# Broadcasting the decay rows of a Mamba-2 mixer: one float32 matmul over a masked product in place of four fp32r matmuls with a selector

## The reference

```python
def ssd_scan(xh, dt, a, bmat, cmat):        # 16 heads, chunks of l = 128 tokens
    ...
    da = (dt * a).reshape(bsz, nc, l, g, hg).transpose(0, 3, 4, 1, 2)
    a_cs = jnp.cumsum(da, axis=-1)
    causal = jnp.tril(jnp.ones((l, l), dtype=bool))
    seg = a_cs[..., :, None] - a_cs[..., None, :]
    decay = jnp.exp(jnp.where(causal, seg, -jnp.inf))
    ...
    y_diag = jnp.einsum('bghcls,bcsghp->bclghp', cb[:, :, None] * decay, x)
    ...
    out_decay = jnp.exp(a_cs).transpose(0, 3, 4, 1, 2)
    y_off = jnp.einsum('bclgn,bcghpn->bclghp', cc, prev) * out_decay[..., None]
```

## Time and profile before

| | |
|---|---|
| median of 3 runs | 3178.87 us (3178.72 to 3179.73) |
| profiled execution | 3178.72 us, span 3177.1 us |
| PE busy | 3030.4 us (95%) |
| DVE busy | 2357.7 us (74%) |
| ACT busy | 1511.5 us (48%) |
| mean granted clock of PE | 0.981 |

### The profile page before, as it was taken

The page is one execution under the profiler, slowest core; times in us unless marked ns, Lnnn a source line. Parts: engine busy times, 40 slices in busy tenths (PEclk is TensorE's granted clock), DMA queues, the critical chain, the costliest instruction groups (busy, mean ns, idle before and its releaser), DMA issues.

```text
span 3177.1 us, 50852 instructions
## 1 busy us (share of the span) xinstructions
PE 3030.4 (95%) x16136; PEld 2531.2 (80%) x16136; DVE 2357.7 (74%) x5175; ACT 1511.5 (48%) x2636; POOL 215.8 (7%) x348
## 2 busy tenths in 40 slices
PE   6999999989998899999999999998999999999998
PEld 4888887769787788877888888877788778888887
DVE  4777787456556766997777777777679977777776
ACT  3222222345753663196555555446532955555544
POOL 0000000000000000092000000000001910000000
PEclk8999999999999999999999999999999999999999
DMA  6333333123222333403555555523343145555553
GB/s 260 108 121 105 114 112 114 68 83 133 79 84 103 107 134 120 157 29 137 191 186 185 186 190 192 196 95 107 133 133 133 41 143 187 185 185 189 191 188 132
DMA packets 73920, 439.61 MB, mean 138 GB/s; under 512 B 7184, under 2 KB 8720, under 8 KB 31824
## 3 DMA queue, kind: packets, MB, share of 16 engines
q1 hardware_dynamic: 71136, 419.15, 38.0%
q0 software_dynamic: 2528, 18.02, 1.6%
q10 hardware_dynamic: 144, 0.98, 0.1%
HBM read 437.08 MB, written 1.05 MB: 138 GB/s over the span
## 4 chain that ended last, share of the span: by engine, by line
PE 77%; DVE 14%; ACT 3%; DVEq 2%; issue 2%; DMA 1%; ACTq 0%; POOL 0%; SPq 0%
PE bank L469 16%; PE bank L471 16%; PE bank L470 16%; PE bank L2323 10%; PE bank L2325 5%; PE bank L1505 2%; DVE arena L2509 2%; PE bank L2286 1%; PE bank L875 1%; DVE arena L2438 1%; DVE arena L2431 1%; DVE arena L2432 1%; PE bank L1225 1%; PE bank L864 1%; PE bank L1243 1%
## 5 line engine op out<-in xcount | busy, mean ns | idle before, releaser
L448 ACT ACTIVATE peer_r<-wring 128x512 fp32r<-128x512 f32 x1280 | 797.6, 631 | 807.1 <-PE bank L471 525.6
L453 DVE TENSOR_TENSOR peer_r<-wring,peer_r 128x512 fp32r<-128x512 f32 x1280 | 869.7, 691 | 413.2 <-ACT peer_r L448 409.9
L2323 PE MATMUL bank<-res_r,peer_r 128*128 128x512 f32 x1408 | 502.8, 397 | 3.4 <-DVE peer_r L453 3.4
L469 PE MATMUL bank<-h_r,peer_r 128*128 128x512 f32 (+1 forms) x1088 | 398.0, 366 | 23.1 <-DVE h_r L664 11.7
L469 PE MATMUL bank<-peer_r 128*128 128x512 f32 x1024 | 404.7, 395 | 2.8 <-DVE peer_r L2540 2.8
L471 PE MATMUL bank<-peer_r 128*128 128x512 f32 x1024 | 401.5, 392 | 0.0
L470 PE MATMUL bank<-peer_r 128*128 128x512 f32 x1024 | 399.6, 390 | 0.0
L2325 PE MATMUL bank<-res_r,peer_r 128*128 128x256 f32 x1408 | 394.9, 280 | 0.0
L471 PE MATMUL bank<-h_r,peer_r 128*128 128x512 f32 (+1 forms) x1088 | 386.1, 355 | 0.0
L470 PE MATMUL bank<-h_r,peer_r 128*128 128x512 f32 (+1 forms) x960 | 335.3, 349 | 0.0
L2323 PEld LDWEIGHTS bank<-res_r,peer_r 128*128 128x128 f32 x1408 | 264.5, 188 | 67.2 <-DVE peer_r L453 4.0
(11 more groups left out here) (390 smaller groups left out, 4566.7 us busy)
## 6 DMA issues: line engine op xcount, KB each, us to landing
wring<-in_w_peer SPq DMA_DIRECT2D x256, 1024.0 KB, 4.9
wring<-in_w_proj SPq DMA_DIRECT2D x34, 1024.0 KB, 4.9
wring<-in_w_hy SPq DMA_DIRECT2D x32, 1024.0 KB, 5.1
arena<-in_w_ada POOLq DMA_DIRECT2D x16, 1024.0 KB, 5.2
wring<-in_w_out SPq DMA_DIRECT2D x16, 1024.0 KB, 4.9
wring<-in_w_ada SPq DMA_DIRECT2D x8, 1024.0 KB, 11.6
wring<-in_w_hyout SPq DMA_DIRECT2D x8, 1024.0 KB, 4.9
wring<-in_w_q SPq DMA_DIRECT2D x8, 1024.0 KB, 4.9
```

The lines of the kernel that those rows point to most:

```text
L448: act.activation(SPLIT[:, buf, 0, :], raw_quarter(name, i, j, q), ACT.Copy).then_inc(split_hi, 1)
L453: v.tensor_tensor(SPLIT[:, buf, 1, :], raw_quarter(name, i, j, q), SPLIT[:, buf, 0, :].bitcast(F32), ALU.subtract).then_inc(split_lo, 1)
L469: pe.matmul(out_ap, w_hi, x_hi, start=start, stop=False, **kw)
L2323: pe.matmul(two_parts(acc[:, :]), SPLIT[:, buf, 0, w], h_both[:, k, :, :], start=(k == 0), stop=False, skip_group_check=True)
```

## The change

`SEL` and `CUM` go, and with them ACT's copy that made the one and DVE's two instructions that made the other. In their place DVE makes `AD`, 16 partitions by 16 blocks of 256: block h holds `cum` on partition h and zero on the other partitions, as the product of `cum` (repeated along the blocks) with the identity (repeated along the tokens), 16x4096 elements in one instruction at the same place in `softplus_rows`. `front_tensor` then takes one float32 matmul with a 16x128 block of ones as weights and the two blocks of its tile (512 columns) as the moving operand. Each column is a sum over 16 partitions of which one isn't zero.

```diff
-        SEL = view(arena_r("sel", c3.at, SSM_HEADS * P)[:, :], SSM_HEADS)
-        c3.take(SSM_HEADS, P)
-        CUM = view(arena_r("cum", c3.at, 2 * T)[:, :], 2)
-        c3.take(2, T)
+        AD = c3.take(SSM_HEADS, T)
...
+        ADP = AD.rearrange("p (n h) t -> p n (h t)", h=2)
...
             if m:
                 pe.wait_ge(ex_ready, m)
-            for hh in range(2):
-                for part in range(2):
-                    mm = pe.matmul(bank[5][:, hh * T:(hh + 1) * T], SEL[0:16, 2 * tile + hh, :], CUM[0:16, part, :],
-                                   start=(part == 0), stop=(part == 1))
-            mm.then_inc(bcast_done, 1)
+            pe.matmul(bank[5][:, :], ones[0:16, :], ADP[0:16, tile, :], start=True, stop=True).then_inc(bcast_done, 1)
...
             act.activation(SROW[0:16, 3, 0:1], LV[l]["a_log"][0:16, :], ACT.Exp).then_inc(alog_out, 1)
-            act.activation(SEL[0:16], wide(ident[0:16, 0:16], 2, P), ACT.Copy)
             act.wait_ge(dec_in, l + 1)
...
             v.drain().then_inc(dec_in, 1)
-            v.tensor_copy(CUM[0:16, 0, :], cum)
-            v.drain()
-            v.tensor_tensor(CUM[0:16, 1, :], cum, CUM[0:16, 0, :].bitcast(F32), ALU.subtract)
+            v.tensor_tensor(AD[0:16], wide(cum, 1, SSM_HEADS), wide(ident[0:16, 0:16], 2, T), ALU.mult)
```

## The result

The changed kernel takes 3198.26 us (median; 3194.56 to 3202.48), the kernel before 3179.3 us in the same comparison: a ratio of 1.0062, with a 95% interval of 1.0050 to 1.0076. That is 19 us slower, and 1.3 us above the upper end of the predicted range. Two things stand out. The loss is half as large again as forecast, and its four times spread over 8 us, where the four of before spread over 1.3.

What follows compares the result with a forecast made beforehand. PE, busy for 95% of the span, was taken as the bound, though it waits for others in the mixer's front half. Delay 5.2, broadcast 5.5 and clock 1.9 added 12.6 us to 3178.72: 3191.3 us, range 3186 to 3197.

Steps and rivals of the forecast that it cites:

- The product: DVE, mixer's front half: the 16x4096 product takes 4.43 us, with nothing back for fewer partitions.
- Its delay after ACT's part in it: Mixer's front half: convolutions start 3.6 us later, ACT absorbs a part, the last sigmoid ends 2.6 and 2.55 us later.
- The idle gap: PE before the gate matmuls: nothing to do for 3.4 us in each mixer.
- The broadcast: PE, mixer's back half: 1.06 us for 0.66, 0.40 more on each of 14 steps, +5.5 us.
- ACT's L1806: Mixer's front half: removing this 1.89 us per layer returns nothing, since ACT then waits 7.70 us for DVE.
- the two terms of work: The front half's delay behind the product, +5.2 us, and the back half's longer broadcast on PE, +5.5 us.
- the paragraph on the clock: Gates on PE: the new idle gap costs one fall to half clock for the two mixers, +1.9 us.
- colder gates: Rival: the gates run wholly at half rate in both mixers, 2 x 3.4 us, giving 3196.2 us; chance 0.08.
- the last sentence of the prediction: Signs of failing: product well under 4 us, broadcast step well under 0.86, or half-clock stretches' sum changing by over two.
- A cheap step: Rival, back half: PE's broadcast pair hides its loads, 0.20 us per tile, giving 3188.6 us; chance 0.14.
- the product is short: Rival, front half: DVE's product takes time by partitions, 0.6 us, no gap opens, giving 3184.2 us; chance 0.03.
- Falls vanish: Rival, back half: the longer broadcast removes all four half-clock stretches, returning 7.6 us, giving 3181.8 us; chance 0.05.

Runs made afterwards that it cites:

- late: The changed kernel with DVE's product moved behind the causal convolutions, where DVE waits for ACT; 3191.1 us, ratio 1.0035.
- before_warm: The kernel before with overwritten float32 matmuls filling PE's idle spots in the mixers' back halves; 3177.43 us, ratio 0.9985.
- after_warm: The changed kernel with overwritten matmuls filling PE's gap before the gates and its idle spots in the back halves; 3184.9 us, ratio 1.0018.
- after_again: The changed kernel run again with no edit; 3197.44 us, ratio 1.0058, its profiled execution 3201.09 us.
- dve_only: The kernel before, old broadcast kept, with an unused 16x3328 product on DVE that starts the convolutions 3.61 us later; 3189.32 us, ratio 1.0037.
- shift_4: The kernel before with four overwritten float32 matmuls (1.7 us) ahead of each mixer's first projection chunk; 3185.86 us, ratio 1.0023.
- shift_8: The kernel before with eight overwritten float32 matmuls (3.5 us) ahead of each mixer's first projection chunk; 3186.01 us, ratio 1.0021.
- inside: The kernel before with each broadcast but tile 0's moved into the next projection chunk, so PE skips waiting for ACT's exponential; 3171.49 us, ratio 0.9976.

## Why the prediction was wrong

**What held.** The product: 4.41 us for 4.43, and nothing back for the fewer partitions. Its delay after ACT's part in it: 2.6 and 2.5 us per mixer for 2.65 and 2.55. The idle gap: 3.38 and 3.28 us for 3.4. The broadcast: 1.05 us for 1.06, on 14 links; 2.95 us per mixer at the full clock, 5.9 us for a forecast 5.5 (14 steps of 0.40 are 5.6, a slip of 0.1 in the text). ACT's L1806 returned nothing: without it the front of `late` is 31.0 us, as before. These are the two terms of work, 11.0 us for 10.7, shown by `before_warm` and `after_warm`.

**What failed.** The step in the paragraph on the clock: "I count one fall for the two mixers: +1.9 us". The median leaves 19.0 - 11.0 = 8.0 us beyond the work, where this term has 1.9. In the two traced executions of the changed kernel 3.7 and 11.4 us are beyond the work, and the mixers' stretches at 0.50 (the table's fronts and backs against those of `after_warm` and `before_warm`) make 2.8 and 9.4 of them: in these traces most of the surplus is the clock. I had looked for its cost only where the change opens a gap. The price of a fall there was right in kind (2.8 us where the trace caught one, between the 1.9 and the 3.4 of the text), but neither of the two mixers of the profiled execution had it. Both had instead a third stretch at 0.50 in the back half, 1.3 us each in the table (86.9 less 82.7, against 82.6 less 79.7); the execution of `after_again` had 18 us at 0.50 in one back half. The text had considered the back half, but only for falls that vanish; that they could be added was missing among the rivals, and so the range ended at "colder gates". Only the last sentence of the prediction names it, as a sign of failing: a sum of the stretches that changes by more than two. In the back halves it went from four to six in the one trace and to seven, beside the one at the gates, in the other.

**Why the falls are added.** The idle gap is not needed (`late` has none, and costs 12 us), and neither is the longer step (`dve_only` and `shift_4` have the old one, and a third stretch). A delay of the work in time is enough, and a delay of twice the size undid it (`shift_4`, `shift_8`). The back half of `before`'s first mixer has seven waits of PE, of 0.5 to 1.9 us. The two delays suggest that whether such a place costs the clock depends on when it comes, and that any change ahead of it can move that; two delays and one trace of each don't show more.

**The rivals.** "Colder gates" happened in one of the four mixers that the two traces of the changed kernel show. "A cheap step" and "the product is short" did not. "Falls vanish" was right that the count is not fixed, with the sign reversed.

**What stays open.** How the 8.0 us of the median divide between gates, back half and the rest of the kernel: only two executions of the changed kernel were traced (14.7 and 22.4 us over the one of before), and each splits differently. Why the same code takes 2842 to 2851 us elsewhere is open too: the trace of `after` needs 3.4 us more than that of `before` up to the first mixer, with as much time at 0.50 between 100 us and there, so the clock is not all of it. Nor was it tested why the changed kernel spreads more widely (3193 to 3203 us over 13 runs) than the kernel before (3176.7 to 3182.3 over 33) with nearly the same thin places. The record only shows that its slower executions have the lower clock: 0.983 in the one of 3193.43 us, 0.981 at 3194.6 and 3195.7, 0.978 or 0.979 in all those above 3198.5.

## What to carry to other kernels

Split a change's cost into work and clock before adding it up: where PE is thinly used in many places, a delay of 2 x 1.7 us cost 6.4 here and one of 2 x 3.45 us 6.6, and two edits' costs didn't add. Compare stages between fixed starts in both traces, at a granted clock of 1.00 (fill the idle spots with matmuls whose result is overwritten, if need be), and give the range a bound for every thin place behind the change, not only for the one that it opens. A large product on VectorE whose result is wanted late belongs behind whatever releases TensorE (`late`: the front lost nothing), and a wait of TensorE for ScalarE in front of a small matmul can be worth more than the matmul's form (`inside`: 8 us, against 6 for the form).

## What the runs showed of the hardware

A float32 matmul of 16 rows and 512 columns keeps PE for 1.05 us, four fp32r ones of 256 columns for 0.66. A product of 4096 elements takes VectorE 4.41 us on 16 partitions and 4.43 on 128. Unexpected was how exactly a stage repeats when the clock is at the same level throughout (79.7 and 82.7 us, in both mixers and across kernels), while the totals of the same kernels spread by 6 to 11 us. The Trainium skill ("TensorE: Matmul & The Clock Gate", section "Why this matters for your kernels") advises against idle gaps between bursts; the traces agree (6.55 us in place of 3.72 for the gates behind a gap of 3.29), but a gap of 3.19 to 3.39 left the clock alone in five other mixers (both of `after`, the first of `after_again`, both of `dve_only`), so the gap's length by itself did not decide. In the back half of `before` the clock fell with no wait of PE longer than 1.9 us.
